# Two-block transformer kernel: query-reversed local attention, with wide key tiles around the maxima of the memory mixer

## Time and profile before

| | |
|---|---|
| median of 3 runs | 1035.52 us (1034.82 to 1035.82) |
| profiled execution: its own time | 1036.81 us |
| profiled execution: span | 1035.1 us, mean granted TensorE clock 0.995 |
| TensorE busy, share of the span | 1017.3 us, 98% |

### The profile page before, as it was taken

One profiled execution on the slowest core, in us unless ns is written; L12 is line 12 of the kernel. 1 busy time (PEld: TensorE's weight loads), 2 busy tenths in 40 slices (PEclk: granted clock), 3 DMA queues, 4 the chain that ended last, 5 costly groups with the idle time before them and its releaser, 6 DMA issues.

```text
span 1035.1 us, 21287 instructions
## 1 busy us (share of the span) xinstructions
PE 1017.3 (98%) x8907; PEld 928.9 (90%) x8907; DVE 748.5 (72%) x1192; ACT 571.4 (55%) x843; POOL 70.9 (7%) x177
## 2 busy tenths in 40 slices
PE   9999999999999999999999999998999999999997
PEld 8778999999987899999998888968899899998885
DVE  5879687788867966778799876766787566555445
ACT  4775586454666558544467674234345456675333
POOL 8600000000000000002140000000000000000000
PEclk9999999999999999999999998999999999999999
DMA  9656554455664555348778440101355356565652
GB/s 324 180 176 186 144 163 133 142 169 175 195 184 126 162 143 161 107 144 250 180 190 208 124 148 23 65 22 43 119 178 173 124 158 179 173 183 188 197 185 82
DMA packets 73551, 160.54 MB, mean 155 GB/s; under 512 B 6917, under 2 KB 16320, under 8 KB 73456
## 3 DMA queue, kind: packets, MB, share of 16 engines
q1 hardware_dynamic: 70304, 150.59, 47.6%
q0 software_dynamic: 2832, 8.06, 4.0%
q10 hardware_dynamic: 320, 0.53, 0.1%
HBM read 158.11 MB, written 1.05 MB: 154 GB/s over the span
## 4 chain that ended last, share of the span: by engine, by line
PE 90%; DVE 4%; ACT 3%; DMA 2%; issue 1%; SPq 0%; POOL 0%; ACTq 0%; DVEq 0%; POOLq 0%
PE psum L472 24%; PE psum L474 24%; PE psum L473 23%; PE psum L891 2%; DMA ring<-in_w_in 2%; PE psum L1037 2%; PE psum L880 1%; PE psum L732 1%; PE psum L710 1%; DVE ring_lo L1443 1%; ACT ring_hi L2511 1%; DVE arena L1629 1%; PE psum L1363 1%; PE psum L724 1%; PE psum L1380 1%
## 5 line engine op out<-in xcount | busy, mean ns | idle before, releaser
L1443 DVE TENSOR_TENSOR ring_lo<-ring,ring_hi 128x1024 fp32r<-128x1024 f32 (+4 forms) x291 | 342.4, 1194 | 163.0 <-ACT ring_hi L2511 161.4
L2511 ACT ACTIVATE ring_hi<-ring 128x1024 fp32r<-128x1024 f32 (+4 forms) x291 | 297.7, 1034 | 249.1 <-PE psum L474 228.1
L472 PE MATMUL psum<-hT,ring_hi 128*128 128x256 f32 x904 | 258.4, 286 | 0.0
L474 PE MATMUL psum<-hT,ring_lo 128*128 128x256 f32 x904 | 254.9, 282 | 0.0
L473 PE MATMUL psum<-hT,ring_hi 128*128 128x256 f32 x904 | 254.5, 282 | 0.0
L472 PEld LDWEIGHTS psum<-hT,ring_hi 128*128 128x128 f32 x904 | 171.6, 190 | 2.4 <-issue 1.0
L473 PEld LDWEIGHTS psum<-hT,ring_hi 128*128 128x128 f32 x904 | 171.6, 190 | 0.0
L474 PEld LDWEIGHTS psum<-hT,ring_lo 128*128 128x128 f32 x904 | 171.6, 190 | 0.0
L472 PE MATMUL psum<-ring_hi,hT 128*128 128x512 f32 (+4 forms) x416 | 156.4, 376 | 2.8 <-DVE ring_lo L1443 2.2
L474 PE MATMUL psum<-ring_hi,hT 128*128 128x512 f32 (+4 forms) x416 | 151.9, 365 | 0.0
L473 PE MATMUL psum<-ring_lo,hT 128*128 128x512 f32 (+4 forms) x416 | 151.6, 364 | 0.0
(11 more groups left out here) (461 smaller groups left out, 1346.3 us busy)
## 6 DMA issues: line engine op xcount, KB each, us to landing
ring<-in_w_in SPq DMA_DIRECT2D x104, 512.0 KB, 3.6
ring<-in_w_ff SPq DMA_DIRECT2D x64, 512.0 KB, 3.6
ring<-in_w_branch SPq DMA_DIRECT2D x24, 512.0 KB, 3.4
ring<-in_w_out SPq DMA_DIRECT2D x24, 512.0 KB, 3.5
ring<-in_w_in SPq DMA_DIRECT2D x24, 384.0 KB, 3.3
ring<-in_w_xkv SPq DMA_DIRECT2D x16, 512.0 KB, 3.7
ring<-in_w_in SPq DMA_DIRECT2D x8, 528.0 KB, 4.0
ring<-in_w_xq SPq DMA_DIRECT2D x8, 512.0 KB, 3.9
```

Of the source, the lines that this page charges most:

```text
L472: mm(b, lhs[0], rhs[0], start=start, stop=False, **how)
L474: return mm(b, lhs[1], rhs[0], start=False, stop=stop, **how)
L1443: V.tensor_tensor(chunk_view(ring_lo, RAW, c), chunk_view(ring, RAW, c), plain(chunk_view(ring_hi, RING_HI, c)), ALU.subtract).then_inc(ev ...
L2511: AC(chunk_view(ring_hi, RING_HI, c), chunk_view(ring, RAW, c), ACT.Copy).then_inc(ev("whi_ready"), 1)
```

```diff
+            def mirrored_turns(name, pieces):
+                b = open_bank(pe, name)
+                for k, piece in enumerate(pieces):
+                    m = mm(b[:, k * P:(k + 1) * P], piece, mirror[:, :], start=True, stop=True)
+                filled(m, name)
...
             def window_scores(i):
-                (t, z, r), (t2, _, r2) = na_pairs[i]
-                pe.wait_ge(ev("bias_ready"), t2 + 1)
                 b = open_bank(pe, ("nas", i))
-                mm(b, mirror[:, :], na_raw[:, t, z:z + 3:2, :] if t == t2 else na_raw[:, :, 4 + z, :], start=True, stop=False,
-                   skip_group_check=True)
                 for k, (t, z, r) in enumerate(na_pairs[i]):
                     o = 64 * z
                     m = mm(b[:, k * S:(k + 1) * S], na_T[o:o + 64, r, t * P:(t + 1) * P], na_T[o:o + 64, 3 + r, :],
-                           start=False, stop=True, skip_group_check=True)
+                           start=True, stop=True)
...
-                        turns(("naT", t, q), [...])
+                        (turns if q else mirrored_turns)(("naT", t, q), [...])
...
             memory_turns(3)
+            window_heads()
+            tiles(keys, 1)
             memory_maxima()
-            window_heads()
+            tiles(keys, 1)
...
-            inverse_level(2, one_tile, two_tiles)
-            one_tile()
+            inverse_level(2, one_tile, one_tile)
             inverse_level(3, one_tile, two_tiles)
...
             def mixed_turns(name, k0, k1):
-                    turns(("yT2", name, t), [...])
+                    (mirrored_turns if name == "na" else turns)(("yT2", name, t), [...])
...
             window_turns(0)
+            next(more_keys)
             window_turns(1)
-            next(more_keys)
...
             def window_maxima(i):
+                if i == 0:
+                    dve.wait_ge(ev("gdv_ready"), 1)
                 b = full(dve, ("nas", i)).rearrange("p (k n) -> p k n", k=2)
-                v(V.tensor_reduce(m2, b, X, ALU.max))
+                if t == t2:
+                    both = na_s[t][:, z, 0:2, :]
+                    v(V.tensor_tensor(both, b, na_raw[:, t, z:z + 3:2, :], ALU.add), free(("nas", i)))
+                    v(V.tensor_reduce(m2, both, X, ALU.max))
+                else:
+                    for k in range(2):
+                        v(V.tensor_tensor(na_s[k][:, z, 2, :], b[:, k, :], na_raw[:, k, 4 + z, :], ALU.add), free(("nas", i)) if k else "dve")
+                    for k in range(2):
+                        v(V.tensor_reduce(m2[:, k:k + 1], na_s[k][:, z, 2, :], X, ALU.max))
...
             inverse_start(1)
-            lo_until(39)
             memory_low(0)
             memory_low(1)
+            lo_until(39)
...
             def window_exp(i):
-                b = full(act, ("nas", i))
-                    a(AC(na_s[t][:, z, r, :], b[:, k * S:(k + 1) * S], ACT.Exp, bias=na_max[:, c:c + 1], accum_out=na_sum[:, c:c + 1]),
+                    a(AC(na_s[t][:, z, r, :], na_s[t][:, z, r, :], ACT.Exp, bias=na_max[:, c:c + 1], accum_out=na_sum[:, c:c + 1]),
-                AC(rtmp[:, 31:32], na_sum[:, 0:1], ACT.Copy).then_inc(free(("nas", i))[0], 1)
...
-            for i in range(6):
+            for i in range(4):
                 window_exp(i)
             hi_until(43)
             copy_out("gdec2", stat_all[:, :], 24)
             delta_factors(0)
+            window_exp(4)
+            window_exp(5)
             delta_factors(1)
-            hi_until(44)
             memory_k(0)
             turned_weights(0)
+            hi_until(44)
             turned_weights(1)
```

More of the change, by code:

```diff
@@ L1130, in window_heads @@
                     for q in range(2):
-                        turns(("naT", t, q), [proj2[:, t, (3 * q + k) * P:(3 * q + k + 1) * P] for k in range(3)])
+                        (turns if q else mirrored_turns)(("naT", t, q), [proj2[:, t, (3 * q + k) * P:(3 * q + k + 1) * P] for k in range(3)])
             def memory_scores():
@@ L1298, in mixed_turns @@
                 for t in range(T):
-                    turns(("yT2", name, t), [y2[:, t, k * P:(k + 1) * P] for k in range(k0, k1)])
+                    (mirrored_turns if name == "na" else turns)(("yT2", name, t), [y2[:, t, k * P:(k + 1) * P] for k in range(k0, k1)])
             more_keys, values = T_steps(("xk", 1), hT), cols_steps(("xv", 0), hT)
             window_turns(0)
+            next(more_keys)
             window_turns(1)
-            next(more_keys)
             window_values(0)
@@ L2860, in window_exp @@
                 act.wait_ge(ev("nas_ready"), i + 1)
-                b = full(act, ("nas", i))
-                for k, (t, z, r) in enumerate(na_pairs[i]):
+                for t, z, r in na_pairs[i]:
                     c = 6 * t + 3 * z + r
-                    a(AC(na_s[t][:, z, r, :], b[:, k * S:(k + 1) * S], ACT.Exp, bias=na_max[:, c:c + 1], accum_out=na_sum[:, c:c + 1]),
+                    a(AC(na_s[t][:, z, r, :], na_s[t][:, z, r, :], ACT.Exp, bias=na_max[:, c:c + 1], accum_out=na_sum[:, c:c + 1]),
                       "nap_ready")
-                AC(rtmp[:, 31:32], na_sum[:, 0:1], ACT.Copy).then_inc(free(("nas", i))[0], 1)
             def delta_factors(t):
```

## The result

The changed kernel takes **1037.99 us**, the median of 22 runs (1035.6 to 1044.28); the kernel before took 1035.58 beside it (22 runs, 1034.17 to 1037.92). The ratio is 1.003, 95% interval [1.0019, 1.0041]: slower by 0.3%. The prediction, 1031.1 and faster, was wrong: the kernel became slower, and 1037.99 is 6.9 us above the forecast.

The account below looks back on a forecast made before the run. TensorE, busy for 98% of the span, was taken to bound the kernel. The terms -0.65 + 0.1 - 4.7 + 0.8 = -4.45 from 1035.52 gave 1031.1 us, range 1027.7 to 1033.8.

Parts of the forecast that it names:

- Stage 1: Up to the first memory turns: memory_low no longer stands behind a weight part and starts earlier, -0.65 us.
- Mirrored products: Three of six turns per row tile become products, +0.8 us between memory_maxima and level 5, again in mixed_turns("na").
- The bank wait at L1024: In memory_maxima: L1024 waits for two small ScalarE copies because window_heads takes banks earlier, +0.7 us.
- Clock at the maxima: Wide work around the 4-row products shortens the half-speed stretch near 636 to 643, half of 3.4 us gained, -1.7.
- +0.3 given back in levels 3 to 5: Levels 3 to 5: TensorE arrives earlier and meets VectorE's bank reads, returning part of the gain, +0.3 us.
- stage 2: From memory_maxima to level 5: products, bank wait, clock and time given back sum to +0.1 us.
- Stage 3: Scores to window_values: six bias products go, -6.3 us, new waits return 1.6, leaving -4.7.
- the waits at L1079, L1198, L1212 and L1269: Between scores and window_values: new TensorE waits of 0.35, 1.15, 1.75 and 0.75 us.
- Half speed in stage 3: Rival: new waits with only 64x64 products and turns between bring the clock down into the wide chunk; 1034.5 us, chance 0.10.
- slower: Rival: half speed feeds on itself from the last gw wait to window_values, losing 6.9 us; 1038.0 us, chance 0.07.

Follow-up runs that it names:

- bias_only: Kernel before, every order kept, with only the mirrored queries, VectorE's adds and the exponentials in place; 1035.82 us, ratio 1.0.
- the heads put back: Changed kernel with window_heads and the key tiles around the maxima as before; 1033.45 us, ratio 0.9981.
- mixed_bias: The heads put back, with the two mixed pairs' bias as two 128x512 TensorE products and VectorE's adds for them gone; 1032.45 us, ratio 0.9964.
- early_adds: The heads put back, with VectorE's adds ahead of reductions and ScalarE's copies of gdec2 and first factors behind two exponentials; 1035.6 us, ratio 1.0007.
- nudge: Changed kernel with the bank rotation moved on by one ahead of memory_states, nothing else; 1035.52 us, ratio 1.002.
- dead_heads: The heads put back, plus the six wide bias products on TensorE as dead work that the scores overwrite; 1038.3 us, ratio 1.0017.
- dead_bias: Changed kernel plus the six wide bias products on TensorE as dead work that the scores overwrite; 1043.53 us, ratio 1.0079.

## Why the prediction was wrong

**The size.** Means of the runs: 1038.90 after and 1035.68 before, 3.2 more. The mean clock fell by 0.9970 - 0.9922 = 0.0048, worth about 5.0 us of 1035. Without that the change would be about 1.7 us faster. Without its term for the clock (-1.7) the forecast was -2.75. So about 1.0 us of the miss lies in work and waits, and 6.7 in the clock: -1.7 forecast, +5.0 measured. The stage table says the same with the half speed taken off (means of two): +3.3 to the scores, -5.0 to `window_values`, -0.7 to the last `state_write`, +0.7 to the end: -1.7.

- *Stage 1, -0.65:* right. The idle is 0.49 instead of 1.14. The working doesn't give it, though: 619.06 - 618.3 is 0.76.
- *Mirrored products, +0.8 twice:* the second measured as 0.7 to the end; the first shows in bias_only, where nothing else differs from before up to the scores: 63.9 us to the scores against 62.7 and 62.8, with half speed and "issue" taken off, so about 1.1.
- *The bank wait at L1024, +0.7:* right, 0.77.
- *Clock at the maxima, -1.7:* in the first pair of profiles it came out so, 7.0 to 3.4 us. But the 7.0 was one execution's. In the six profiles with a tile on either side of the maxima, the mean loss there is 1.7 us (3.4, four of 1.7, and 0); in the eight without it is 2.1 (three of 3.4, four of 1.7, and 0). The term is about -0.4, and its sign is not sure.
- *+0.3 given back in levels 3 to 5:* the failed step of stage 2. I counted the banks on as far as L1024 and then bounded the rest by VectorE's load. Two banks of levels 4 and 5 now meet VectorE's late reads, 0.84 and 1.57: 2.4. With half speed and "issue" taken off, the scores start about 3.1 us later after L952 than before. Of these the heads put back take away 2.5, by removing bank waits of 3.2 (0.77, 0.84 and 1.57); 0.15 are the forecast (0.8 - 0.65), and about 0.5 stays unexplained.
- *Stage 3, -4.7:* right as far as the work and the waits go. Over the eight profiles without wide products the stage takes 26.2 us with 3.4 at half speed, 27.8 with 6.8 and 29.1 with 10.2 (means), which runs back to an estimated 24.7 with none. The forecast was 29.7 - 4.7 = 25.0. The waits at L1079, L1198, L1212 and L1269 came within 0.35 of their terms; the one at L1187 (0.9) was missed. One sign was added up wrongly: by its own terms (4.7 and 0.55) `window_values` had to start about 5.2 us earlier, not 4.8.
- *No term for the clock in stage 3:* the step that failed most. The sum takes the six wide products off at their full length and puts the clock there at 1.00. Half speed took 3.4 us of the stage in both executions, none before, and in the first another 5.1 behind it.

**The rivals.** "Half speed in stage 3" and "slower" together had 0.17. The 3.4 us that half speed took of stage 3 is what the first of them names. Its place is earlier than either says: in after the clock falls at `gdec2`, in bias_only among the scores. The 1038.0 of the second is luck. It wants 6.9 us lost in the stage and turns that make later copies; half of that was lost there, no run shows the feedback, and bank waits and half speed outside the stage made up the rest. I argued against it from rows 13, where the clock held through a wait and the turns. What those rows don't have is the stretch ahead of them without wide products; before, six of these stood in the 15.8 us that precede it. Behind the scores no profile with the products, six or two, falls up to `window_values` (six of six), and every one without them does (eight of eight).

The Trainium skill, "TensorE: Matmul & The Clock Gate", Part 1, says that the clock follows how busy TensorE has lately been. Behind the scores the traces agree: TensorE was busy for 26.65 of 29.9 us with dead work and no fall, for 8.52 of 10.8 us ahead of the first fall there in after. At the maxima they don't: before, TensorE was busy for 2.13 of 2.20 us ahead of the fall, with products of 4 rows. The Trainium skill, Part 4 of the same page, says that transposes don't count as a busy TensorE in the same way. The runs here don't decide that: in mixed_bias the window turns run from 699.29 on, with waits of 1.36 and 0.48 us, and the stretch stays at 1.00; in early_adds the clock falls at 700.4, between turns, in the wait of 3.00 us.

**What stays open.** Why a stretch of 10.3 us at half speed begins near `window_values` in three executions (after, nudge, mixed_bias) and in no other, and whether it is the width of the products or the waits they cover that holds the clock: in all of mixed_bias, dead_heads and dead_bias the products also cover the waits at L1079, L1187 and L1198, and no kernel had wide work with these waits left in. The fall in bias_only speaks for the width: it came behind a single wait of 0.92 us since the start of the scores, while before held the clock through one of 1.30. That doesn't settle it.

## What to carry to other kernels

Wide products that look like waste on a busy TensorE can be what keeps the work around them at full speed, so before such work is moved to another engine, ask what is left in that stretch. That doesn't make dead work pay: six dead products cost 3.7 us net here. Wide work that saves another engine something is the better choice. With two of six such products the ratio is 0.9964, with none 0.9981, in intervals that overlap. When an operation that takes banks is moved, count the banks on to the next place where the rotation comes round to the old order, not only to the first wait. And where a term rests on one stretch at half speed, look at a second execution: its length was 7.0 us in one and about 3.4 in the other.

## What was not expected of the hardware

Two executions of one program differ by 10.7 us of 1035 (spans of 1042.5 and 1031.8), more than any single edit here moved a median. Half speed makes 6.8 of these. The runs of a kernel go with the clock: after runs from 1035.6 us at a mean clock of 0.996 to 1044.28 at 0.988.

ScalarE's exponentials by line in the changed kernel, duration in ns (min/median/max):

```profile
L2877 ACT ACTIVATE proj<-proj,na_max x6: 507/508/509, 688.6 to 695.5; 128x256 f32<-128x256 f32 x6
```

From SBUF they take 0.508 us against 0.474 from PSUM: 0.034 more, between the 0.022 of the nearest row and the 0.043 that follow, as an estimate, from the Trainium skill, "VectorE: DVE Perf Modes", section on the TRN2 errata.
